# Layer 0 attention: keys and values prepared once for the four heads that share them

## The reference, cut to what matters

```python
q = rms_norm(q.reshape(b_, t, B_KV_HEADS, B_GROUP, B_HEAD_DIM), q_g)   # 2 groups of 4 heads
k = rms_norm(k.reshape(b_, t, B_KV_HEADS, B_HEAD_DIM), k_g)            # 2 key heads
qr    = rope_2d(q, row, col)                                           # latent tokens only
k_all = concatenate([rope_2d(k, row, col), ctx_k], axis=1)
v_all = concatenate([v, ctx_v], axis=1)
s = einsum('bqhgd,bshd->bhgqs', qr, k_all) * scale
p = softmax(s)
y_b = einsum('bhgqs,bshd->bqhgd', p, v_all) * silu(g_b)
```

## Time and profile before

| | before |
|---|---|
| median of 3 runs | 2545.57 us (2542.26 to 2546.54) |
| the profiled execution | 2546.45 us |
| its span, first to last instruction | 2544.8 us |
| mean granted PE clock | 0.986 of full speed |
| PE busy | 2424.3 us (95%) |
| DVE busy | 1648.3 us (65%) |
| ACT busy | 909.3 us (36%) |
| POOL busy | 406.4 us (16%) |

### The profile page before, as it was taken

One profiled execution on the slowest core, in us unless ns is written; L12 is line 12 of the kernel. 1 busy time (PEld: TensorE's weight loads), 2 busy tenths in 40 slices (PEclk: granted clock), 3 DMA queues, 4 the chain that ended last, 5 costly groups with the idle time before them and its releaser, 6 DMA issues.

```text
span 2544.8 us, 37204 instructions
## 1 busy us (share of the span) xinstructions
PE 2424.3 (95%) x11818; PEld 1964.4 (77%) x11818; DVE 1648.3 (65%) x2952; ACT 909.3 (36%) x2096; POOL 406.4 (16%) x465
## 2 busy tenths in 40 slices
PE   5899999999999999999999999999999999999996
PEld 2578888877777778878887787777878888877885
DVE  5456777887877457766456665565666666654876
ACT  3122333333333222223244444454444444432223
POOL 0001122222212100000112222222221222101000
PEclk9999999999999999999999999999999999999998
DMA  9955555554444556644432233333233333247666
GB/s 364 339 165 166 161 172 164 164 183 133 143 149 166 197 185 200 218 173 145 144 103 81 94 96 101 102 105 100 81 101 97 108 101 109 91 160 236 191 202 226
DMA packets 166170, 395.52 MB, mean 155 GB/s; under 512 B 15057, under 2 KB 15697, under 8 KB 161041
## 3 DMA queue, kind: packets, MB, share of 16 engines
q1 hardware_dynamic: 135680, 259.57, 31.3%
q0 software_dynamic: 30352, 134.23, 15.5%
HBM read 332.93 MB, written 63.18 MB: 156 GB/s over the span
## 4 chain that ended last, share of the span: by engine, by line
PE 68%; DVE 14%; DVEq 6%; ACT 5%; issue 4%; DMA 2%; SPq 1%; ACTq 0%; POOL 0%; POOLq 0%
PE ps L629 54%; PE ps L536 3%; PE ps L527 3%; DVE w_lo L1332 3%; PE ps L514 3%; DVE small L1217 2%; DVE ada_sum L1362 1%; DVEq L1355 1%; DMA w_raw<-in_w_ada_dram 1%; DVEq L1439 1%; ACT w_hi L932 1%; DVE wT_lo L1208 1%; PE ps L616 1%; PE ps L645 1%; DVEq L1215 1%
## 5 line engine op out<-in xcount | busy, mean ns | idle before, releaser
L629 PE MATMUL ps<-w_hi,hT_hi 128*128 128x512 f32 x2760 | 1125.4, 408 | 22.4 <-DVE stage L1349 9.0
L629 PE MATMUL ps<-w_hi,hT_lo 128*128 128x512 f32 x2760 | 1085.0, 393 | 0.0
L629 PE MATMUL ps<-w_lo,hT_hi 128*128 128x512 f32 x2760 | 1082.8, 392 | 0.0
L629 PEld LDWEIGHTS ps<-w_hi,hT_hi 128*128 128x128 f32 x2760 | 523.5, 190 | 124.2 <-issue 16.6
L629 PEld LDWEIGHTS ps<-w_hi,hT_lo 128*128 128x128 f32 x2760 | 520.9, 189 | 115.5
L1332 DVE TENSOR_TENSOR w_lo<-w_raw,w_hi 128x512 fp32r<-128x512 f32 x544 | 404.1, 744 | 312.1 <-ACT w_hi L932 302.3
L629 PEld LDWEIGHTS ps<-w_lo,hT_hi 128*128 128x128 f32 x2760 | 523.2, 190 | 87.4 <-issue 1.4
L932 ACT CAST w_hi<-w_raw 128x512 fp32r<-128x512 f32 x544 | 335.6, 619 | 443.5 <-PE ps L629 431.0
L1362 DVE SCALAR_TENSOR_TENSOR ada_sum<-w_raw,cond,ada_sum 128x512 f32<-128x512 f32 x480 | 365.8, 803 | 32.4 <-issue 7.5
L1217 DVE TENSOR_REDUCE small<-ps 128x1 f32<-128x640 f32 (+1 forms) x200 | 143.7, 718 | 59.6 <-PE ps L527 42.9
L860 ACT ACTIVATE work<-ps,small 128x640 f32<-128x640 f32 (+1 forms) x120 | 85.3, 711 | 242.5 <-DVE small L1217 242.5
(11 more groups left out here) (196 smaller groups left out, 2319.9 us busy)
## 6 DMA issues: line engine op xcount, KB each, us to landing
w_raw<-in_w_in_dram SPq DMA_DIRECT2D x208, 512.0 KB, 3.9
w_raw<-in_w_ada_dram SPq DMA_DIRECT2D x256, 256.0 KB, 3.1
z<-stage POOLq DMA_DIRECT2D x27, 1280.0 KB, 5.2
w_raw<-in_w_out_dram SPq DMA_DIRECT2D x64, 512.0 KB, 4.3
work<-z POOLq DMA_DIRECT2D x72, 320.0 KB, 3.8
work<-in_w_ada_dram SPq DMA_DIRECT2D x24, 512.0 KB, 11.6
w_raw<-in_w_ada_dram SPq DMA_DIRECT2D x24, 512.0 KB, 11.4
work<-o POOLq DMA_DIRECT2D x8, 1280.0 KB, 7.1
```

Of the source, the lines that this page charges most:

```text
L629: last = nc.tensor.matmul(ps[:, t, :], x[:, kt, t * P:(t + 1) * P], w[:, kt % RING, :], start=(kt == 0 and i == 0), stop=(kt == KT - 1 and ...
```

## The change

Keys and values are handled by the first head of each group alone (heads 0 and 4, called fresh). For the other six heads the piece r = 1 is gone; r = 2 transposes only the context tile of the query and follows r = 0 at the slot that r = 1 had; semaphores are counted up by 2 there so that the numbering stays. The value split is gone too, and so are the norm and rotation of keys, the loads of keys and values and the store of the context keys. Pair 3 loads the keys and values of the second group. Where PE waited for modulation columns ahead of r = 2, non-fresh heads of pairs 1 to 3 wait ahead of the first S. The loops over pairs are split on PE, ACT and DVE: 0, a loop over 1 and 2 (PE: 1 to 3), 3, 4, a loop over 5 and 6, 7. POOL's loops stay.

```diff
+def without_keys(order):
+    return order[:2] + order[3:]
...
-                last.then_inc(s.t_ready, 1)
+                last.then_inc(s.t_ready, 1 if fresh or q != 1 else 2)
...
                 pe.wait_ge(s.s_exp, h * NS + (n + 1))
+                if n == 0 and not fresh and not tiles:
+                    pe.wait_ge(mod_free, h + 3)
...
+                    elif r == 1 and not fresh:
+                        blocks = [q_in[:, TS, :]]
                     elif r == 1:
                         blocks = [k_in[:, t, :] for t in range(TS)]
...
-                    if p == 0:
-                        pe.wait_ge(s.v_split, h + 1)
+                    if p == 0 and fresh:
+                        pe.wait_ge(s.v_split, h // KV_HEADS + 1 if L.n == 0 else h + 1)
...
-            with pe.Fori(0, 4) as i:
-                pair0(i, pace0)
+            pair0(0, pace0, fresh=True)
+            with pe.Fori(1, 4) as i:
+                pair0(i, pace0k, without_keys(ORDER0))
             pe.wait_ge(tables_in, 16 * 3)
-            with pe.Fori(4, 7) as i:
-                pair0(i, pace0s, ORDER0S, [i - 4])
-            pair0(7, pace0t, ORDER0T, [3, 4], ada=False)
+            pair0(4, pace0s, ORDER0S, [0], fresh=True)
+            with pe.Fori(5, 7) as i:
+                pair0(i, pace0sk, without_keys(ORDER0S), [i - 4])
+            pair0(7, pace0tk, without_keys(ORDER0T), [3, 4], ada=False)
...
-                    if r == 3 and L.maps == 1:
+                    if r == 3 and L.maps == 1 and fresh:
                         value_hi()
-                    turn(r, pieces[r])
-                    r += 1
+                    turn(r, pieces[r] if fresh or r != 1 else q_pieces[1])
+                    r += 1 if fresh or r != 1 else 2
...
-            for n, (z, g) in enumerate(((q_in, gq), (k_in, gk))):
+            for n, (z, g) in enumerate(heads):      # heads: queries, and keys only if with_keys
...
-                for z in (q_in, k_in):
+                for z in (q_in, k_in)[:2 if with_keys else 1]:
...
                 next_qk(L0, i + 1)
-                next_v(L0, i + 1)
+                if next_fresh:
+                    wait(kn_stored, 16)
+                    load_keys(1)
+                    wait(S[0].v_split, 1)
+                    load_v(L0, KV_HEADS)
...
-                rotate_head(L0, i + 1)
+                rotate_head(L0, i + 1, next_fresh)
```

More of the change, by code:

```diff
@@ L488, in wait_slot_used, with attention_pe @@
                 eng.wait_ge(w_used, (c - 1) * 15 + (KT + k + 1 + W_CREDIT))
[L491 removed]
+        def attention_pe(pe, L, h, order=None, tiles=(), fresh=True):
             s = S[L.n]
@@ L571, in attention_pe @@
                     turn(q, blocks)
-                    r, q = r + 1, q + 1
+                    passed = 1 if fresh or r != 1 else 2
+                    r, q = r + passed, q + passed
                 elif kind == "S":
@@ L769, in _, with pair0 @@
             project_chunk(C_L0 + 2, 2, finish_at(2, 0, False))
-            def pair0(i, pace, order=None, tiles=(), ada=True):
-                steps = attention_pe(pe, L0, i, order, tiles)
+            def pair0(i, pace, order=None, tiles=(), ada=True, fresh=False):
+                steps = attention_pe(pe, L0, i, order, tiles, fresh)
                 step = stepper(steps, pace)
@@ L846, in turn @@
                         last = nc.scalar.activation(dst, src, ACT.Copy, scale=scale)
-                last.then_inc(s.t_hi, 1)
+                last.then_inc(s.t_hi, 1 if fresh or r != 1 else 2)
             def scores(n, u, src, width):
@@ L912, in attention_act @@
                         value_hi()
-                    if n == 4 and L.maps == 1 and not last_head:
+                    if n == 4 and L.maps == 1 and next_fresh:
                         square_next(1, k_in)
@@ L1021, in _, with pair0 @@
                 evacuate(i + (C_L0 + 1), i + 1)
-            def pair0(i, pace, evac, order=None, last_head=False):
-                steps = attention_act(act, L0, i, order, last_head)
+            def pair0(i, pace, evac, order=None, last_head=False, fresh=False, next_fresh=False):
+                steps = attention_act(act, L0, i, order, last_head, fresh, next_fresh)
                 split_chunk(i + C_P0, stepper(steps, pace))
@@ L1195, in heads_dve, with attention_dve @@
                 yield from attention_dve(dve, L1, first + x, before=norm_out(dve, first + x))
-        def attention_dve(dve, L, h, order=None, tiles=(), last_head=False, before=None):
+        def attention_dve(dve, L, h, order=None, tiles=(), last_head=False, before=None, fresh=True, next_fresh=False):
             s = S[L.n]
@@ L1593, in _, with pair0 @@
             finish(first_norm)
-            def pair0(i, pace, gate=False, order=None, tiles=(), last_head=False, ada=None):
-                steps = attention_dve(dve, L0, i, order, tiles, last_head)
+            def pair0(i, pace, gate=False, order=None, tiles=(), last_head=False, ada=None, fresh=False, next_fresh=False):
+                steps = attention_dve(dve, L0, i, order, tiles, last_head, None, fresh, next_fresh)
                 first = second = None
@@ L1609, in pair0 @@
                         ada_tile(ada, tile)
[L1611 to L1615, removed]
+            pair0(0, pace0, ada=A1 + 2, fresh=True)
+            with dve.Fori(1, 3) as i:
+                pair0(i, pace0k, order=without_keys(ORDER0), ada=i + (A1 + 2))
+            pair0(3, pace0k, order=without_keys(ORDER0), ada=A1 + 5, next_fresh=True)
+            pair0(4, pace0s, True, ORDER0S, [0], ada=A1 + 6, fresh=True)
+            with dve.Fori(5, 7) as i:
+                pair0(i, pace0sk, True, without_keys(ORDER0S), [i - 4], ada=i + (A1 + 2))
+            pair0(7, pace0tk, True, without_keys(ORDER0T), [3, 4], last_head=True)
             scale_columns()
```

92 lines of the change are left out of this document (53 added, 39 removed).

## The result

| | before | after |
|---|---|---|
| median | 2545.74 us (6 runs, 2542.26 to 2553.52) | 2532.41 us (6 runs, 2529.19 to 2535.82) |
| span of the profiled execution | 2544.8 us | 2531.8 us |
| mean granted PE clock | 0.986 | 0.988 |
| PE, DVE, ACT, POOL busy | 2424, 1648, 909, 406 us | 2414, 1608, 891, 356 us |

The ratio is 0.9943, with a 95% interval of 0.9929 to 0.9957: the change makes the kernel 13.3 us faster. The forecast was 2526 us in a range of 2518 to 2536. The time lies in that range, and the gain is two thirds of the 19.5 us that were forecast.

A forecast was written before the change was run, and what follows sets the result against it. PE, busy for 95% of the span, was taken to bound the kernel. Transposes 2.0, chunk ends 13.6, T stop 2.2 and a half-speed stretch 1.7 sum to 19.5 us, giving 2526 us, range 2518 to 2536 us.

The forecast's parts named there:

- Transposes: Term 1, on PE: six heads lose six transpose blocks each, 4.0 us, of which 2.0 us counted directly (heads 1 to 3).
- The ends of chunks 4 to 6: Term 2: without POOL's second rotation DVE empties banks earlier, bank stops and half-speed stretches go; gain 13.6 us.
- The new stops: PE waits ahead of the first scores of heads 5, 6 and 7, about 1.5 us each; sign: 1 to 2 us.
- Nothing late for the scores: Rival, chunk ends: DVE reaches banks earlier, PE's own work sets the distance; term 2 is 17.8 us, 2522 us; chance 17%.
- the full 5.7 us: Chunk ends, by the lock rule: DVE could win back all the time POOL's second block held the port, not 3.2 us.
- The bank stop stays: Rival, chunk ends: DVE is late through its own ada tiles or transfers; gain 8.2 us, 2537 us; chance 10%.
- only transposes: Rival: stops move to the next wait, half-speed stretches return elsewhere; gain 4.0 us, 2541.6 us; chance 6%.
- The T stop of pairs 5 and 6: Term 3: without the value split the 2.2 us stop halves to 1.1 us; gain 2.2 us, plus 1.7 us half-speed stretch.
- Pair 4 is a fresh head and keeps its stop.: Under term 3: the T stop in pair 4 was to stay at 2.2 us.
- Edits at nothing: Key norm, squares and rotation in pairs 0 to 2, splits of heads 1 to 3, loads and moved waits: no gain counted.
- Slower, by code: Rival: split loops make PE stop for code at pairs' borders, at worst 6.8 us each; up to 2574 us; chance 3%.
- The main case: All terms hold, 2526 us; half-speed stretches behind new stops or in pairs 4 and 6 vary it, 2522 to 2533; chance 61%.

The follow-up runs named there:

- half_rotation: Kernel before, with one part of the change alone: POOL rotates no keys in pairs 4, 5 and 6; 2539.39 us, ratio 0.9956.
- keys_rotated: Changed kernel, with POOL still doing a second rotation, of the unread key buffer, in pairs 4, 5 and 6; 2547.83 us, ratio 0.9999.
- after_again: Changed kernel measured and traced once more with no edit; 2532.07 us, ratio 0.9931.
- norm_later: Changed kernel, with the norm of the gating tile begun one piece later on DVE (from r = 5, not r = 4); 2527.83 us, ratio 0.9931.
- keep_step: Changed kernel, with the query norm finished one DVE step later where no keys are normed, as before the change; 2529.15 us, ratio 0.9916.
- split_loops: Kernel before, with only the change's split of the loops over pairs, same instructions in the same order; 2543.28 us, ratio 0.9995.
- two_edits_tile: Changed kernel, with query norm one step later in pairs 0 to 2, gating norm one piece later, one ada tile moved to weight tile 5; 2518.80 us, ratio 0.9885.

## Why the prediction was right, and where not

*Transposes.* Right: 36 fewer. Pair 3, during which POOL still rotates queries and keys for the next head, is 0.93 us shorter; 0.66 us was forecast.

*The ends of chunks 4 to 6.* Right in mechanism and size. The banks are reached 3.5 us earlier (3.2 forecast), the stop ahead of the scores took the place of the bank stop, and the stretch is 22.3 us in all (23.1). half_rotation shows it with this part alone, and keys_rotated by putting it back: the bank stops return, if smaller in two of three cases. The new stops averaged 0.9 us, not 1.5: both DVE and PE reached the scores within a few tenths of what was read, and the stop is the difference of the two. One of them, 0.66 us, lies below the 1 to 2 us that the prediction named as its sign. "Nothing late for the scores" falls, and with it the full 5.7 us that the prediction had read out of the lock rule of the Trainium skill (SBUF — State Buffer, Who interferes with whom): with the second block gone DVE won 3.5 us. The slow `w_lo` beside POOL agrees with the rule; whether the loser waits for the whole instruction no run here shows. "The bank stop stays" and "only transposes" fall by the same rows.

*The T stop of pairs 5 and 6.* Right: 1.00 and 0.99 us (1.1 forecast), and no half-speed stretch.

*"Pair 4 is a fresh head and keeps its stop."* This failed: 3.8 to 4.25 us. The stop had been read as DVE's own chain alone. The gating norm in that chain waits for a load, and before the change that load landed with 0.94 us to spare. After, it landed 2.6 us later, the norm began 1.7 us later in the pair, and 1.55 us reached PE. Cost: 1.6 us of stop, and 1.1 us for the longer half-speed stretch (in after_again 1.75 us and nothing). norm_later shows the chain. The load was issued 1.3 us later behind one late write of a store, most likely held up by a code fetch; why that strikes some kernels and not others, and why the load itself took 1.35 us longer, is open.

*"Edits at nothing" in pairs 0 to 2.* This failed in sign. The prediction looked at what the missing key work frees and not at what it starts sooner. Pairs 0 to 2 were forecast 1.3 us shorter and are 2.2 us longer. With keep_step they are 5.8 us shorter than that. This is 3.6 us below before, 2.3 us more than the transposes explain, which the prediction had not counted either.

*Slower, by code.* Fell with split_loops.

*The range.* The main case was said to give 2522 to 2533 us, but its own terms (1.7 us less, or 1.7 and 5 us more than 2526) give 2524 to 2533 us. The range up to 2536 us was made for half-speed stretches and for bank stops that stay in part. What used it up was something else: 3.5 us in pairs 0 to 2 and 2.7 us in pair 4, against 1.5 us better than forecast in the other pairs. That part of the hit is luck.

## What to carry to other kernels

Before counting a removed step as free, ask what it lets begin sooner, and what runs on the engine next door at that time: here a GpSimd rotation (POOL) that became half as long cost 4 us where it slid forward onto VectorE (DVE) work that the matrix engine needed, and won most of the change where it drew away from such work. When a stop of the bounding engine ends with a chain on another, list every wait in the chain, those that are just met too: a transfer with a microsecond of slack is the next stop. After a change of load, look again at orders written by hand; two steps of one engine, each moved by one place, won 14.2 us in the pairs, as much as the change.

## What the runs showed of the hardware that was not expected

The traces list the 16 KB code fetches among the packets of the transfer engines. In pair 4 they took 0.95 to 0.97 us in ten traces and 1.6 us in two (after_again, two_edits_tile), and stores during which one ran had a late last write far more often (25 of 67, against 7 of 245). Stops of PE of 1.0 to 1.7 us were not followed by the lower clock level in pairs 0 to 2 and 5 to 7 of the changed kernel; of the three stops of 2.2 us in the kernel before, two were and one was not, and a stop of 3.8 us had 6.8 us at the lower level behind it in one execution and 3.4 us in another (after_again, stop of 3.99 us). One stretch at the lower level had no stop of 0.1 us or more in the 12 us ahead of it. Windows of half_rotation in pair 1:

```profile
344.00:348.00 4.00, 4.00 (x28) 3.30 (x27) 2.71 (x5) 1.43 (x3) 0.00 (x0) 1.00 0.98 313
348.40:351.80 3.40, 3.40 (x12) 2.73 (x11) 1.54 (x4) 1.10 (x2) 0.56 (x1) 0.51 1.00 364
```

PE is busy throughout, and the clock is at 0.51 for 3.4 us. That pair lasted 71.85 us against 70.19 before, which is 1.7 us of the pair sum of that kernel.
